# Router logits taken from the unnormalised x, x turned once into the output banks, and the norm weight multiplied in where columns are copied

## The chip, the cores and the metric

The kernel runs on one core of one Trainium2 chip. The time is device microseconds of one execution. The core has a matrix engine (TensorE, in the profile PE, its weight loads PEld), VectorE (DVE), ScalarE (ACT), GpSimd (POOL) and SyncE (SP), which here only issues transfers; all transfers share 16 DMA engines. All data is fp32.

## What is computed

One layer of a hybrid decoder over 264 tokens (256 of a prompt, 8 samples) of width 1024. The change touches only the part behind the mixer: the residual, the norm before the experts, the router and the experts' inputs.

```python
x = x + m                                        # m: output of the mixer
h = _rmsnorm(x, norm_ffn_g)                      # y = x * rsqrt(mean(x*x) + EPS) * g
gp = softmax(h @ w_router_group)                 # 4 groups, the best one is taken
el = (h @ w_router_expert)                       # 32 experts, 8 of them in the best group
tv, ti = top_k(softmax(el of that group), 2)     # two experts for a token
for e in range(32):
    a = silu(h @ w_expert_gate[e]) * (h @ w_expert_up[e])
    out = out + combine[:, e:e + 1] * (a @ w_expert_down[e])
x = x + out                                      # then a last RMSNorm, and the output
```

Every expert has three matrices of 1024x512 or 512x1024, 2 MB each: 192 MB for the 32 experts.

## The kernel before

**Stages.** Up to about 332 us the kernel runs the mixer. Its last projection, label `wo`, makes eight 128x264 tiles; VectorE adds each to the turned residual `xT` (features on partitions, L1404). The router, the sorting of tokens and the first gather fill 332 to 351 us. Then 16 pairs of experts follow, 26.8 us each on TensorE: `gate`, `up` (both in `hidden`, L2007), `turn`, `down` (L2045) and `combine` (L2053).

**The router before.** VectorE also makes `hT[d] = xT[d] * g` (L1407), which raises `xg_ready`. TensorE's `route` multiplies `hT` with the router's weights `wrout` (L1918) into `logits`. ScalarE squares `xT`, VectorE sums the squares, and TensorE sums them over partitions into one column for each token tile (L1929). From it ScalarE and GpSimd make the factor `rs` for each token. `turn_groups` turns `hT` to token-major (L1581, six groups of four transposes), and ScalarE copies these groups times `rs` to `xrow` (L1026), which SyncE stores as `tok_rows`. In between, `seat` multiplies `xT` with the identity into banks 0 to 3 (L1933), where the experts' outputs are added up until the end; the fourth and fifth group of seats stand behind the ranks. VectorE picks the best group and two experts by `first_max` (five steps each, L1422 to L1426), makes `member`, TensorE counts ranks from it (`ranks`, L1957 to L1961), and VectorE turns the ranks into positions and the selection matrices `sel0` (L1450, L1451).

**The first gather.** `first_block` (L1971) multiplies `xrow` with `sel0`, half by half, into two banks. `m_gathered` counts the halves. Here ScalarE copies the columns of the first pair of experts to `xe` (L1075, L1076) and all columns to `xall` (L1077). For pairs 1 to 15 GpSimd copies from `xall` to `xe` (L793).

**The weights' ring.** SyncE's queue is written by hand: it streams the experts' matrices into a ring of 20 half slots of 1 MB (`RING`, `load_half`, `load_slot`, L556, L559, L569), and its instructions wait in order. The places that the mixer frees last are four half slots over the arrays `gates` and `x_early`; halves 16 to 19 go there. Half 18 lies over `xT`, half 17 over the router's small arrays (freed by `smalls_done`, L1475), half 19 over `xrow` (freed by `m_gathered` 2 and by `rows_kept`, the landing of `tok_rows`). From half 20 on a load waits for the TensorE step that read its place last. The queue there is:

```python
load_half(16)
sp.wait_ge(*misc.read(("ht", 5)))
... two stores of tok_rows
sp.wait_ge(seated, 1); sp.wait_ge(x_kept, 1)
load_half(18)
sp.wait_ge(quad_ready, 1)
... two stores of tok_quad
sp.wait_ge(smalls_done, 1)
load_half(17)
sp.wait_ge(rows_kept, 32); sp.wait_ge(m_gathered, 2)
load_half(19)
```

Ahead of load 7 (one whole slot) SyncE also stores `hT` to `h_rows` (L591). Only a branch for overfull experts reads it back, and that branch is not taken.

## Time and profile before

| | |
|---|---|
| median of 3 runs | 806.62 us (805.08 to 806.87) |
| the profiled execution's own time | 806.2 us |
| its span | 804.2 us |
| TensorE busy | 773.9 us (96%) |
| VectorE, ScalarE, GpSimd busy | 234.4, 176.4, 97.2 us |
| moved by DMA | 267.90 MB, mean 333 GB/s over the span |
| chain that ended last, by engine | PE 81%, DMA 13%, DVE 2% |

A span is what the profiler saw between the first and the last instruction; the time of an execution is 2.0 us more here. A small "idle before" of TensorE does not say that transfers have slack: read the share of the DMA engines in the same stretch beside it. L12 is line 12 of the kernel before.

### The profile page before, as it was taken

What the parts mean: (1) busy time and instruction counts of PE and PEld (TensorE: products, weight loads), DVE (VectorE), ACT (ScalarE), POOL (GpSimd) and SP (SyncE); (2) the same over time, 40 slices, a digit from 0 to 9 for tenths busy, and PEclk for the clock granted to TensorE, in tenths of its full rate; (3) what the DMA queues carried; (4) which work ended last, traced back from release to release, by engine and by line L of the source; (5) the groups of instructions that cost most, each with busy time, mean ns of one, the idle gap of its engine ahead of it and who ended that gap; (6) DMA issues with size and microseconds to landing.
All of it is one profiled execution on the core that took longest, in us unless ns stands there. A gap on an engine that the chain in (4) does not pass through costs nothing.

```text
span 804.2 us, 10140 instructions
## 1 busy us (share of the span) xinstructions
PE 773.9 (96%) x4170; PEld 445.8 (55%) x4170; DVE 234.4 (29%) x533; ACT 176.4 (22%) x321; POOL 97.2 (12%) x128
## 2 busy tenths in 40 slices
PE   8999999999999999999999999999999989999995
PEld 7888887888888888863333333333333333333331
DVE  4099869482550322441101110111011101101112
ACT  3104333657544101231111001100110010010011
POOL 5300064523300000001101000001000000000001
PEclk9999999999999999999999999999999999999998
DMA  9845586578849974499999999999999999999993
GB/s 329 244 149 187 164 239 207 181 214 169 276 148 365 398 259 191 162 360 430 423 429 417 426 429 425 429 426 427 427 429 427 430 427 429 425 428 419 421 409 149
DMA packets 76374, 267.90 MB, mean 333 GB/s; under 512 B 5598, under 2 KB 37578, under 8 KB 63647
## 3 DMA queue, kind: packets, MB, share of 16 engines
q1 hardware_dynamic: 74402, 264.13, 84.3%
q10 hardware_dynamic: 1461, 1.45, 0.6%
q0 software_dynamic: 464, 1.64, 0.5%
q8 instruction: 35, 0.57, 0.3%
q14 instruction: 12, 0.10, 0.0%
HBM read 259.13 MB, written 8.55 MB: 333 GB/s over the span
## 4 chain that ended last, share of the span: by engine, by line
PE 81%; DMA 13%; DVE 2%; issue 1%; ACT 1%; POOL 1%; SPq 0%; DVEq 0%
PE bank L2007 23%; PE bank L1630 23%; PE bank L2045 10%; PE bank L1903 7%; PE bank L2053 6%; DMA slots<-in_w_expert_gate_dram 5%; DMA x_early<-in_w_expert_gate_dram 5%; DMA slots<-in_w_expert_down_dram 2%; PE bank L1850 2%; PE bank L1740 1%; DMA slots<-in_w_in_dram 1%; PE bank L2034 1%; DVE x_early L1488 1%; PE bank L1971 1%; PE bank L1662 1%
## 5 line engine op out<-in xcount | busy, mean ns | idle before, releaser
L1630 PE MATMUL bank<-hT,slots 128*128 128x264 f32 x832 | 189.6, 387 | 0.0
L2007 PE MATMUL bank<-slots,hT 128*64 128x512 f32 x624 | 177.9, 601 | 2.1 <-DMA slots<-in_w_expert_gate_dram 2.1
L1630 PEld LDWEIGHTS bank<-hT,slots 128*128 128x128 f32 x832 | 156.6, 190 | 26.8 <-issue 0.6
L1488 DVE TENSOR_TENSOR x_early<-x_early,bank 128x512 f32<-128x512 f32 x16 | 11.0, 688 | 376.6 <-PE bank L2007 376.6
L2007 PEld LDWEIGHTS bank<-slots,hT 128*64 128x64 f32 x624 | 55.1, 138 | 91.1 <-issue 86.5
L2045 PE MATMUL bank<-slots,wrep 128*64 128x512 f32 x304 | 85.4, 595 | 4.7 <-ACT wrep L1053 4.0
L2007 PE MATMUL bank<-slot,hT 128*64 128x512 f32 x208 | 81.4, 593 | 0.0
L793 POOL COPY hT<-x_early 128x512 f32 x30 | 17.9, 623 | 369.3 <-PE bank L2007 286.2
L2053 PE MATMUL bank<-hT,diag 128*128 128x512 f32 x128 | 59.2, 605 | 0.2 <-ACT hT L1065 0.2
L2045 PEld LDWEIGHTS bank<-slots,wrep 128*64 128x64 f32 x304 | 26.0, 137 | 49.3 <-issue 39.6
L1228 DVE SCALAR_TENSOR_TENSOR slot<-slot,rows_buf 128x256 f32<-128x256 f32 x120 | 49.4, 488 | 0.0
L1053 ACT COPY wrep<-bank 128x512 f32<-128x512 f32 x16 | 9.4, 586 | 169.6 <-PE bank L2034 169.6
L2045 PE MATMUL bank<-slot,wrep 128*64 128x512 f32 x112 | 42.7, 596 | 2.3 <-ACT wrep L1053 2.3
L2007 PEld LDWEIGHTS bank<-slot,hT 128*64 128x64 f32 x208 | 24.9, 137 | 34.9 <-issue 33.7
L2007 PE MATMUL bank<-x_early,hT 128*64 128x512 f32 x96 | 42.3, 594 | 1.5 <-DMA x_early<-in_w_expert_gate_dram 1.5
L2053 PEld LDWEIGHTS bank<-hT,diag 128*128 128x128 f32 x128 | 22.9, 189 | 35.7 <-issue 35.1
L2007 PE MATMUL bank<-gates,hT 128*64 128x512 f32 x96 | 42.5, 594 | 0.0
L1065 ACT COPY hT<-bank 128x512 f32<-128x512 f32 x31 | 16.7, 589 | 113.3 <-PE bank L2045 113.3
L1048 ACT ACTIVATE x_early<-bank 128x512 f32<-128x512 f32 x16 | 16.9, 1057 | 109.2 <-PE bank L2007 109.2
L1903 PE MATMUL bank<-gates,slots 128*128 128x264 f32 x128 | 30.1, 390 | 0.0
L1903 PE MATMUL bank<-x_early,slots 128*128 128x264 f32 x128 | 28.6, 386 | 0.0
L1903 PEld LDWEIGHTS bank<-x_early,slots 128*128 128x128 f32 x128 | 24.3, 190 | 4.2
(301 smaller groups left out, 759.6 us busy)
## 6 DMA issues: line engine op xcount, KB each, us to landing
slots<-in_w_expert_gate_dram SPq DMA_DIRECT2D x15, 2048.0 KB, 23.2
slots<-in_w_expert_up_dram SPq DMA_DIRECT2D x15, 2048.0 KB, 28.7
slots<-in_w_expert_down_dram SPq DMA_DIRECT2D x15, 2048.0 KB, 29.7
slots<-in_w_in_dram SPq DMA_DIRECT2D x13, 2048.0 KB, 10.0
slots<-in_w_expert_gate_dram SPq DMA_DIRECT2D x10, 1024.0 KB, 26.2
slot<-in_w_expert_gate_dram SPq DMA_DIRECT2D x5, 2048.0 KB, 27.7
slot<-in_w_expert_up_dram SPq DMA_DIRECT2D x5, 2048.0 KB, 23.7
slot<-in_w_expert_down_dram SPq DMA_DIRECT2D x5, 2048.0 KB, 34.1
```

What stands on the lines that cost most here:

```text
L793: pool.tensor_copy(xe[:, :, e * SLOTS:(e + 1) * SLOTS], xall[:, :, bass.ds(at[e], SLOTS)]).then_inc(m_xe, 1)
L1048: se.activation(act.rearrange("s (f c) -> s c f", f=FT), bank[GATE][:, :].rearrange("s (c f) -> s c f", f=FT), ACT.Silu).then_inc(m_silu, 1)
L1053: se.copy(actT, bank[4][:, :].rearrange("p (f s) -> p f s", f=FT)).then_inc(m_actT, 1)
L1065: se.copy(ytok[:, 512 * i:512 * (i + 1)], bank[4 + i][:, :]).then_inc(m_ytok, 1)
L1228: i = dve.scalar_tensor_tensor(conv[:, c, 0:SEQ], upad[:, c, j:j + SEQ], taps[:, c, j:j + 1], conv[:, c, 0:SEQ], ALU.mult, ALU.add)
L1488: dve.tensor_tensor(act.rearrange("s (f c) -> s f c", f=FT), act.rearrange("s (f c) -> s f c", f=FT), bank[UP][:, :].rearrange("s (c f) -> ...
L1630: last = mm(out, w[:, a, t * P:(t + 1) * P], (hT if c else xgain)[:, a, :], start=(a == 0), stop=(a == KT - 1))
L1850: last = mm(bank[proj.bank(("ya", d))][:, 0:T], w[:, c, d * P:(d + 1) * P], conv[:, c, :], start=(c == 0), stop=(c == CT - 1))
L1903: last = mm(bank[proj.bank((label, d))][:, 0:T], w[:, a, (d % 4) * P:(d % 4 + 1) * P], src[:, a, :], start=(a == 0), stop=(a == KT - 1))
L2007: last = mm(out[sl, :], xe[:, a, sl], expert_view(p, kind, e, a // 2)[:, a % 2, :], start=(a == 0), stop=(a == KT - 1))
L2045: last = mm(bank[4 + i][sl, :], actT[:, f, sl], expert_view(p, 2, e, f)[:, 0, 512 * i:512 * i + 512], start=(f == 0), stop=(f == FT - 1))
L2053: return mm(bank[Y_BANKS[t][i]][:, :], wc[:, t * P:(t + 1) * P], ytok[:, CHUNK * i:CHUNK * (i + 1)], start=False, stop=stop)
```

## The change

The norm's weight g is multiplied into `wrout` once (128x288, on VectorE, before the first `wo` tile is taken), so that `route` reads `xT` itself. `hT`, its eight multiplications and the store `h_rows` are gone. `xT` is turned once, by transposes, straight into banks 0 to 3, where it stays as the residual; ScalarE takes the rows for `xrow` from those banks. Only the 8 samples are turned into the ring of banks 6 and 7. The sum over partitions is made 128 columns wide instead of one. `xrow` now lacks g; so g comes in again where columns are copied to `xe`: on VectorE for pair 0 (`first_columns`), on GpSimd for pairs 1 to 15, where the copy becomes a multiplication. g in the features' order (`g_by`, 128x8) comes by a small transfer. The choice of two experts is made with VectorE's `max` (eight largest of a row) and a key built from the experts' numbers. In SyncE's queue halves 18, 19 and 17 are loaded in another order and after other waits.

```diff
@@ SyncE
-                if c == WO + 1:
-                    sp.wait_ge(xg_ready, KT)
-                    sp.dma_start(h_rows[:, :, :], hT[:, :, :]).then_inc(h_stored, 16)
                 sp.wait_ge(proj.ready, proj.written(stream[c][1]))
                 load_slot(n)
+                if n == 5:
+                    sp.dma_start(g_by, ins["norm_ffn_g"][0].rearrange("(p a) -> p a", p=P)).then_inc(g_by_in, 16)
             load_half(16)
-            sp.wait_ge(*misc.read(("ht", 5)))
-            sp.dma_start(tok_rows[0:SEQ, :].rearrange("(t p) d -> p t d", p=P), xrow[:, 0:2, :]).then_inc(rows_kept, 16)
-            sp.dma_start(tok_rows[SEQ:T, :], xrow[0:NB, 2, :]).then_inc(rows_kept, 16)
-            sp.wait_ge(seated, 1)
+            sp.wait_ge(misc.ready, misc.written(("ht", 5)))
             sp.wait_ge(x_kept, 1)
             load_half(18)
+            sp.wait_ge(row_made, 4)
+            sp.dma_start(tok_rows[0:SEQ, :].rearrange("(t p) d -> p t d", p=P), xrow[:, 0:2, :]).then_inc(rows_kept, 16)
+            sp.wait_ge(*misc.read(("ht", 5)))
+            sp.dma_start(tok_rows[SEQ:T, :], xrow[0:NB, 2, :]).then_inc(rows_kept, 16)
             sp.wait_ge(quad_ready, 1)
...
-            sp.wait_ge(smalls_done, 1)
-            load_half(17)
             sp.wait_ge(rows_kept, 32)
             sp.wait_ge(m_gathered, 2)
             load_half(19)
+            sp.wait_ge(smalls_done, 1)
+            load_half(17)
             load_half(NR)
@@ GpSimd
                 for e in range(2):
-                    pool.tensor_copy(xe[:, :, e * SLOTS:(e + 1) * SLOTS], xall[:, :, bass.ds(at[e], SLOTS)]).then_inc(m_xe, 1)
+                    pool.tensor_tensor(xe[:, :, e * SLOTS:(e + 1) * SLOTS], xall[:, :, bass.ds(at[e], SLOTS)],
+                                       g_by[:, :].unsqueeze(2).broadcast_to([P, KT, SLOTS]), ALU.mult).then_inc(m_xe, 1)
@@ ScalarE
-            for i in range(6):
+            for i in range(4):
                 t, half = i // 2, i % 2
...
+                se.wait_ge(y_seated, i + 1)
+                se.activation(xrow_by[:, t, :, SLOTS * half:SLOTS * half + SLOTS],
+                              bank[Y_BANKS[t][half]][:, :].rearrange("p (q a) -> p a q", a=KT), ACT.Copy,
+                              scale=rs[:, t:t + 1]).then_inc(row_made, 1)
...
-            se.wait_ge(h_stored, 16)
-            se.wait_ge(offs_ready, 1)
-            second = se.value_load(offs[0:1, 1:2], min_val=0, max_val=SLOTS)
             for j in range(2):
-                se.wait_ge(m_gathered, j + 1)
+                se.wait_ge(first_xe, 2 * j + 2)
                 src = bank[GATHER[j]][:, :].rearrange("p (a c) -> p a c", a=4)
-                se.copy(xe[:, 4 * j:4 * j + 4, 0:SLOTS], src[:, :, 0:SLOTS]).then_inc(first_xe, 1)
-                se.copy(xe[:, 4 * j:4 * j + 4, SLOTS:], src[:, :, bass.ds(second, SLOTS)]).then_inc(first_xe, 1)
                 se.copy(xall[:, 4 * j:4 * j + 4, 0:P], src).then_inc(m_xall, 1)
@@ VectorE
+            dve.wait_ge(wrout_in, 32)
+            dve.tensor_tensor(wrout[:, :, :], wrout[:, :, :], vec[:, 60:60 + KT].unsqueeze(2).broadcast_to([P, KT, NG + NE]), ALU.mult).then_inc(router_ready, 1)
...
-                dve.wait_ge(*proj.read(("wo", d)))
-                dve.tensor_scalar(hT[:, d, :], xT[:, d, :], vec[:, 60 + d:61 + d], None, ALU.mult).then_inc(xg_ready, 1)
...
+            def first_columns(j):
+                dve.wait_ge(m_gathered, j + 1)
+                src = bank[GATHER[j]][:, :].rearrange("p (a c) -> p a c", a=4)
+                gain = g_by[:, 4 * j:4 * j + 4].unsqueeze(2).broadcast_to([P, 4, SLOTS])
+                dve.tensor_tensor(xe[:, 4 * j:4 * j + 4, 0:SLOTS], src[:, :, 0:SLOTS], gain, ALU.mult).then_inc(first_xe, 1)
+                dve.tensor_tensor(xe[:, 4 * j:4 * j + 4, SLOTS:], src[:, :, bass.ds(second, SLOTS)], gain, ALU.mult).then_inc(first_xe, 1)
@@ TensorE
-                pe.wait_ge(xg_ready, a + 1)
+                pe.wait_ge(*proj.read(("wo", a)))
...
+            def seat(t, i):
+                for c in range(4):
+                    last = mm(bank[Y_BANKS[t][i]][:, c * P:(c + 1) * P], xT[:, 4 * i + c, t * P:(t + 1) * P], ident[:, :],
+                              start=(c == 0), stop=(c == 3), is_transpose=True)
+                last.then_inc(y_seated, 1)
```

`first_columns(0)` stands on VectorE behind `quad_ready`, `first_columns(1)` behind the flag and ahead of the steps that end in `smalls_done`; a register load of an offset stands before both.

On TensorE, the place is the stretch from the sum over partitions to the first gather. Before (`hT` and `x_early` are the normalised and the raw x, `gates` holds `member`, the 1-column product is the end of the sum):

```order
L1929 MATMUL bank<-ones,rows_buf 128x1 x2
L1929 MATMUL bank<-ones,rows_buf 8x1
L1581 MATMUL bank<-ident,hT 128x128 x8
L1933 MATMUL bank<-ident,x_early 128x128 x4
L1581 MATMUL bank<-ident,hT 128x128 x8
L1933 MATMUL bank<-ident,x_early 128x128 x4
L1581 MATMUL bank<-ident,hT 8x128 x8
L1957 MATMUL bank<-gates,tri 128x64
L1958 MATMUL bank<-gates,ones 128x64
L1959 MATMUL bank<-gates,ones 128x96
```

Now:

```order
L1945 MATMUL bank<-ident,x_early 128x128 x4
L1953 MATMUL bank<-ones,rows_buf 128x128 x2
L1953 MATMUL bank<-ones,rows_buf 8x128
L1945 MATMUL bank<-ident,x_early 128x128 x12
L1967 MATMUL bank<-ident,x_early 8x128 x8
L1977 MATMUL bank<-gates,tri 128x64
L1978 MATMUL bank<-gates,ones 128x64
L1979 MATMUL bank<-gates,ones 128x96
L1980 MATMUL bank<-gates,tri 128x32
L1981 MATMUL bank<-gates,ones 128x32
L1989 MATMUL bank<-x_early 128x128 x24
```

The sixteen transposes of `hT` and eight of the sixteen seat products ahead of the ranks have become sixteen transposes; the eight seat products that stood between the ranks and the gather (L1971 before, L1989 now) are gone from there.

On VectorE, the choice of the experts, from the masked logits on. Before, the second `first_max` and the start of the third (`gates` holds all small arrays):

```order
L1422 TENSOR_REDUCE gates<-gates 128x3
L1423 TENSOR_TENSOR gates<-gates 128x96
L1424 TENSOR_TENSOR gates<-gates,desc 128x96
L1425 TENSOR_REDUCE gates<-gates 128x3
L1426 TENSOR_TENSOR gates<-desc,gates 128x96
L1434 SCALAR_TENSOR_TENSOR gates<-gates 128x96
```

Now, the whole choice up to `member` (L1442):

```order
L1432 MAX gates<-gates 128x8 x3
L1435 SCALAR_TENSOR_TENSOR gates<-gates,desc 128x32
L1436 SCALAR_TENSOR_TENSOR gates<-gates,desc 128x32
...
L1438 SCALAR_TENSOR_TENSOR gates<-gates 128x96
L1440 MAX gates<-gates 128x8 x3
L1442 TENSOR_TENSOR gates<-gates 128x96
```

Twelve dependent steps of 96 elements (five, one, five and `member`) have become three `max`, six steps of 32 elements that don't wait for each other, one of 96, three `max` and `member`.

On SyncE, the queue from load 6 on (L569 and L559 are loads of weights; the L559 into `gates` is half 16, the one into `x_early` half 18):

```order
-L569 DMA slots<-in_w_expert_gate_dram 128x4096
-L591 DMA h_rows<-hT 128x2112
-L569 DMA slots<-in_w_expert_gate_dram 128x4096
+L592 DMA x_early<-in_norm_ffn_g_dram 128x8
+L569 DMA slots<-in_w_expert_gate_dram 128x4096 x2
 L559 DMA gates<-in_w_expert_up_dram 128x2048
-L596 DMA tok_rows<-x_early 128x2x1024
-L597 DMA tok_rows<-x_early 8x1024
 L559 DMA x_early<-in_w_expert_up_dram 128x2048
+L598 DMA tok_rows<-x_early 128x2x1024
+L600 DMA tok_rows<-x_early 8x1024
```

Behind the two stores of `tok_quad` the queue has half 17 (into `gates`) and half 19 (into `x_early`): before 17, then 19; now 19, then 17.

One store of 1056 KB is gone, half 18 has moved ahead of the stores of rows, and half 19 ahead of half 17.

## Rows read from the trace of the kernel before

**Rows 1.** Chain that ended last, its end: start us, us, what.

```profile
770.86 18.95 DMA slots<-in_w_expert_down_dram
...
789.86 1.94 PE bank L2045 x8
...
798.01 0.66 DVEq L1536
```

**Rows 2.** Waits of TensorE from 250 us on: total us, times, longest.

```profile
PE bank L2007 <- DMA slots<-in_w_expert_gate_dram: 2.1, 1, 2.1
...
PE bank L2007 <- DMA x_early<-in_w_expert_gate_dram: 1.5, 1, 1.5
...
PE bank L2045 <- DMA slots<-in_w_expert_down_dram: 0.6, 1, 0.6
```

**Rows 3.** Windows: engines' busy us, PEclk, DMA share, GB/s at a row's end.

```profile
334.00:350.00 16.00, 15.27 (x114) 14.26 (x114) 11.42 (x52) 7.82 (x18) 0.88 (x1) 0.89 0.99 380
350.00:352.00 2.00, 2.00 (x15) 1.02 (x15) 1.94 (x4) 1.25 (x4) 0.00 (x0) 1.00 0.50 62
352.00:786.00 434.00, 416.74 (x1896) 146.28 (x1894) 46.45 (x81) 46.83 (x71) 24.57 (x41) 1.00 1.01 425
```

**Rows 4.** Timeline of SyncE's DMA issues: start us, us.

```profile
332.59 0.34 SPq L591 DMA_DIRECT2D h_rows<-hT  x1
...
341.49 0.38 SPq L596 DMA_DIRECT2D tok_rows<-x_early  x1
...
349.53 0.34 SPq L559 DMA_DIRECT2D gates<-in_w_expert_up_dram  x1
```

**Rows 5.** DMA issues by line: KB each, us to landing.

```profile
h_rows<-hT SPq DMA_DIRECT2D x1, 1056.0 KB, 4.9
```

**Rows 6.** Chain that ended last, from router to first gather.

```profile
332.21 0.37 DVE hT L1407
...
332.62 0.92 PE bank L1918 x6
...
333.59 0.70 PE bank L1929 x6
...
334.30 1.60 PE bank L1581 x8
...
339.74 0.87 PE bank L1581 x8
...
340.61 0.17 PE bank L1957 x2
...
344.52 6.17 PE bank L1971 x48
```

**Rows 7.** Timeline of VectorE and ScalarE in the router.

```profile
335.09 0.25 DVE L1422 TENSOR_REDUCE gates<-gates 128x3 f32<-128x96 f32 x1
...
335.73 1.27 ACT L1026 ACTIVATE x_early<-bank,rs 128x512 f32<-128x512 f32 x2 [1.00 <-POOL rs L772]
...
338.29 0.26 DVE L1436 TENSOR_TENSOR gates<-gates 128x96 f32<-128x96 f32 x1
...
348.92 0.19 DVE L1472 SCALAR_TENSOR_TENSOR gates<-gates 128x32 f32<-128x32 f32 x1
```

**Rows 8.** Windows with the granted clock low.

```profile
336.00:338.00 2.00, 2.00 (x11) 2.00 (x11) 1.76 (x7) 0.99 (x2) 0.00 (x0) 0.50 0.90 313
```

**Rows 9.** Chain: 30 matmuls of L2007 after two waits, and pair 1's first.

```profile
381.61 13.88 PE bank L2007 x64
...
650.90 8.78 PE bank L2007 x30
...
709.62 7.08 PE bank L2007 x30
```

**Rows 10.** GpSimd by form: busy us, mean ns.

```profile
L714 POOL TENSOR_TENSOR slots<-slots,wrep 120x512 f32<-120x512 f32 x2 | 2.5, 1264 | 7.1 <-DMA wrep<-in_conv_dw_w_dram 7.1
```

**Rows 11.** Timeline of GpSimd before pair 1.

```profile
378.96 1.16 POOL L793 COPY hT<-x_early 128x512 f32 x2 [16.19 <-ACT x_early L1041]
```

More of the change, by code:

```diff
@@ L227, in hybrid_layer @@
         gmax, gpos, gsum, gval = small(1), small(1), small(1), small(1)
-        elm, eq, elm2 = (small(NE) for _ in range(3))
+        elm, key, elm2 = (small(NE) for _ in range(3))
         oh = flat(6 * NE).rearrange("p (k a n) -> p k a n", k=2, a=3)
@@ L231, in hybrid_layer @@
         oh1, oh2 = oh[:, 0], oh[:, 1]
-        e1, p1, e2, p2, ed, er, den, rec = (small(1) for _ in range(8))
+        ed, er, den, rec = (small(1) for _ in range(4))
+        top, chosen = (flat(24).rearrange("p (a n) -> p a n", a=3) for _ in range(2))
         comb, member = small(NE), small(NE)
@@ L763, in _ @@
             pool.memset(dflat[:, T:], 0.0).then_inc(c_const, 1)
-            pool.wait_ge(proj.ready, proj.written(("wo", KT - 1)))
-            pool.wait_ge(xg_ready, KT)
+            pool.wait_ge(*proj.read(("wo", KT - 1)))
             pool.tensor_copy(x_samples, xT[:, :, SEQ:T]).then_inc(x_kept, 1)
@@ L1928, in _ @@
             for i, (t0, m) in enumerate(TOK_TILES):
-                last = mm(bank[misc.bank("ms")][0:m, i:i + 1], rstd[:, t0:t0 + m], ones[:, 0:1], start=True, stop=True)
+                last = mm(bank[misc.bank("ms")][0:m, i * P:(i + 1) * P], rstd[:, t0:t0 + m], ones[:, 0:P], start=True, stop=True)
             last.then_inc(M_ready, 1)
-            def seat(t, i, last=False):
-                for c in range(4):
-                    turned = mm(bank[Y_BANKS[t][i]][:, c * P:(c + 1) * P], xT[:, 4 * i + c, t * P:(t + 1) * P], ident[:, :],
-                                start=(c == 0 and not last), stop=(c == 3 and last))
-                return turned
             def seat_samples(x):
@@ L1941, in seat_samples @@
                        start=False, stop=False, tile_position=(0, at))
-            def beside_rows(t, half):
-                if t and half == 0:
-                    pe.wait_ge(*proj.read(("wo", KT - 1)))
-                    seat(0, t - 1)
-            turn_groups(misc, "ht", hT, beside_rows)
+            for t, i in ((0, 1), (1, 0), (1, 1)):
+                seat(t, i)
+            for half in range(2):
+                misc.before_write(pe, ("ht", 4 + half))
+                out = bank[misc.bank(("ht", 4 + half))]
+                for c in range(4):
+                    last = tr(out[0:NB, c * P:(c + 1) * P], xT[:, 4 * half + c, SEQ:T], ident[:, :])
+                last.then_inc(M_ready, 1)
             pe.wait_ge(member_ready, 1)
@@ L2146, in _ @@
                     for i in range(2):
-                        seat(t, i, last=True).then_inc(y_sum, 1)
+                        for c in range(4):
+                            last = mm(bank[Y_BANKS[t][i]][:, c * P:(c + 1) * P], xT[:, 4 * i + c, t * P:(t + 1) * P], ident[:, :],
+                                      start=False, stop=(c == 3))
+                        last.then_inc(y_sum, 1)
                 mm(bank[GATE][:, 0:PART], ident[:, :], sample_sum, start=True, stop=False)
```

103 lines of the change are left out of this document (58 added, 45 removed).

## The prediction

> **What bounds the kernel now.** I read the end of the chain that ended last first, because a change in the middle counts only by what it does to the end. There the last load of expert weights is issued at 770.86, lands 18.95 us later, and TensorE starts on it at 789.86 [rows 1]. One half slot is 1.05 MB, which takes 2.5 us at the rate below, so those 19 us are a queue: the DMA engines, not the issue, are late. Then the windows: from 352 to 786 the DMA share is 1.01 at 425 GB/s, while TensorE is busy for 416.7 of 434 us, nearly full as well [rows 3]. The waits show how close the two are: behind 250 us TensorE waited for weights three times, 2.1, 1.5 and 0.6 us [rows 2]. The third is the last load. So the transfers are the bound by a little: the end is the moment at which the stream becomes continuous, plus a fixed volume over a fixed rate, plus a tail from 789.86 on that the change leaves alone. TensorE is some 4 us behind them.
>
> The stream becomes continuous late. From 334 to 350 the share is 0.99 but only at 380 GB/s, and from 350 to 352 the queue is nearly dry: share 0.50, 62 GB/s [rows 3]. It starts again with half 17, issued at 349.53 when `smalls_done` came [rows 4]. Half 19 waits for the end of the first gather, 344.52 + 6.17 = 350.69 [rows 6], and follows it while half 17 is still moving.
>
> **What the change does to TensorE and VectorE (the time of the first gather's end).**
> Removed multiplication of `hT`: the last logits waited for its 0.37 us at 332.21 [rows 6]; they start at 332.2 in place of 332.62, a gain of 0.4. The g in `wrout` costs a VectorE operation of 288 elements, some 0.45 us, under the first tile of `wo`, for which VectorE waits anyway: nothing.
> TensorE up to the ranks, before: 340.61 - 332.62 = 8.0 us [rows 6]. Now: logits 0.9; the sum, 0.7 for six narrow passes [rows 6], which I keep for 128 columns; sixteen transposes; eight small ones. Eight transposes took 1.60 us at granted clock 0.50 (0.20 each) and the eight small ones 0.87 at full clock (0.11 each) [rows 6, 8]. So sixteen and eight cost 1.8 + 0.9 at the full clock, 3.2 + 1.6 if all of it is at half. Half speed lasted for part of it only, so I take 1.4 us on top at most. TensorE is free at 332.2 + 0.9 + 0.7 + 2.7 = 336.5, or 337.9.
> VectorE up to `member`, before: 335.09 to 338.55, 3.5 us, for twelve steps of 0.29 [rows 7]. Now: a step of 32 elements is 0.19 us [rows 7], back to back I take 0.15; `max` has no row, and I price it like such a step (bounds: 0.1, and 0.3 like a step of 96). Three `max` 0.5, six steps 1.0, one of 96 0.3, three `max` 0.5, `member` 0.3: 2.6 us, bounds 2.3 to 3.5. `member` is ready at 338.55 - 0.4 - 0.9 = 337.2. The two `is_equal` behind it (0.5 us) lie under TensorE's ranks.
> The ranks thus start at 337.2 if TensorE keeps its clock, at about 338.0 if not: 3.4 or 2.6 us earlier than 340.61. From there to the end of the gather it is 350.69 - 340.61 = 10.1 us in the same steps. ScalarE must have made six rows by then: pairs of them take 1.27 [rows 7], begun at about 335.9 they end at 339.7, ahead of the gather. The gather would end at 347.3 or 348.1.
>
> **The clock.** The seats between ranks and gather are gone, so TensorE now has nothing for about 2.6 us there (340.61 plus 1.2 of ranks to 344.52, less 0.1). After its wait of 2.1 us the 30 matmuls of L2007 took 8.78 us, after the wait of 1.5 us the same 30 took 7.08 [rows 2, 9]: one stretch at the low clock cost 1.7 us. The low level was also granted from 336 to 338, behind the narrow products of the router [rows 8]; that is 1.2 of 2.4 GHz. A gap of 2.6 us is longer than the one that cost 1.7, so I give the gather a good half chance to pay the 1.7.
> The Trainium skill, page "TensorE: Matmul & The Clock Gate", section on the HAM clock gate, says the same thing as a rule: after idleness the array gets half its pulses, and a monitor that runs free of the program decides, so that it differs from run to run; its formula for the penalty (throttled time times one half) is what rows 9 show. By that rule the seats' work was worth more than nothing where it stood, which speaks against this change. Were the rule certain to bite both times, the gather would end at 349.8.
>
> **What it does to the transfers.** Removed: a store of 1056 KB [rows 5], 1.08 MB, 2.5 us of stream at 425 GB/s. Load 7 goes out some 1.2 us earlier, since it stood behind the store issued at 332.59 [rows 4] and behind the multiplication that the store waited for. Both would be worth 3.7 us if the stream were continuous from there. It isn't. Load 7, half 16, half 18 and the rows are 5.3 MB, 13 to 14 us at 380 to 425 GB/s: begun at about 332.5 they are through at 346. The next load is now half 19, and its wait is the end of the gather, 347.3 to 349.8. The room that the store leaves turns into an idle gap in front of half 19. What counts is when the stream starts again: 349.53 before, the gather's end now. The gather's gain g (350.69 less the new end) is thus worth only g - 1.16 (350.69 less 349.53). `rows_kept` is no later: rows are through at 346, and their landing has a microsecond or two.
> Half 17 behind it needs `smalls_done`. That comes after `first_columns(1)`: two copies out of PSUM with g, about 0.45 each, then about 1.1 us of small steps, so 2.0 us behind the gather. Half 19 covers 2.5 us: no second gap, with 0.4 to spare.
> The register load on VectorE (the one at the end of the kernel took 0.66 [rows 1]; bounds 0 and 1.3) delays `quad_ready` but stands in the 3 us in which the gather's first half runs.
> GpSimd: 128x512 as a product costs about 1.26 instead of 0.58: 120x512 took that, and two copies 1.16 [rows 10, 11]. For pair 1: 378.96 + 2.5 = 381.5, the gate starts at 381.61 [rows 9]: 0 to 0.3 us on TensorE, which has slack. Later pairs have 5 us and more.
> The small transfer of g stands where the DMA engines are free: nothing.
>
> **Sum**, against the profiled execution's 806.2, which is 0.4 under the median of 806.62: g is 3.4 with no low clock, 2.6 or 1.7 with one stretch, 0.9 with both. End: -2.2; -1.4 or -0.5; +0.3.
>
> **Forecasts and rivals.**
> Main case, one stretch at the low clock, 0.40: -0.9, so 805.7 by the median (804.9 to 806.4 for its own terms).
> No low clock in the way, 0.25: -2.2, 804.4. For it: the sum is now 128 columns wide, which keeps TensorE busier; against it: the gap of 2.6 us.
> Both, 0.15: +0.3, 806.9.
> Rival 1, the transfers are not the bound or the store's 2.5 us do count, 0.08: then TensorE's 2.6 to 3.4 or the stream's 3.7 us come through, 803.3. Against it: rows 1 and the dry window.
> Rival 2, slower, 0.08: VectorE. `smalls_done` now stands behind the gather, and SyncE's whole queue behind half 17 waits for it. Decisive point: 2.5 us behind the gather. If the products with the broadcast g, the register load or the small steps take longer, each microsecond more is one of stream lost. With both low clocks (+0.3) and 2 us over that point it is +2.3, 808.9.
> Rival 3, nothing of the router's part gets shorter since something else (ScalarE's rows, the width of the sum) ends last, 0.04: g = 0, +1.2, 807.8.
>
> **How the numbers follow.** A measurement here tells 0.2%, 1.6 us, from no change. Faster than that: most of the second case and rival 1, 0.25 x 0.8 + 0.08 = 0.28, with a little of the main case's lower end 0.31. Slower: rival 2 and some of the third case and rival 3, 0.12. The same: 0.57. The range from 803.6 to 808.0 leaves out half of rival 1, rival 2 and some noise.
>
> **What would show it.** The DMA share of the stretch ahead of half 19's issue: a clear gap, longer than before. The issue of half 19 within 0.1 us of the gather's last product, half 17 some 2.0 behind. `member` about 1.3 us earlier; the ranks 2.6 to 3.4. The granted clock in the gather: 0.5 somewhere in it, and the gather then nearer 7.9 than 6.2 us. From there on share 1.0, and TensorE's waits for weights over 5 us in sum instead of 4.2. I am wrong if the end moves by more than the moment at which the stream starts again, if that moment is set by `smalls_done`, or if there is no gap in the transfers ahead of half 19.

## The result, and the profile of the changed kernel

The changed kernel took 808.57 us, median of 22 executions (804.86 to 812.95); the kernel before took 805.81 (804.95 to 806.87, 22 executions beside them). The ratio is 1.0036, with a 95% interval from 1.0026 to 1.0047: slower by 2.8 us, which is small but clear of the noise. The median is outside the range of 803.6 to 808.0, and it moved the other way: my 805.7 stood for 0.9 us less than the 806.62 that I had as the median before. The spread has grown too, from 1.9 us to 8.1, and it goes with TensorE's mean granted clock: twelve executions with 0.990 to 0.993 took 804.9 to 808.6 us, ten with 0.982 to 0.987 took 809.0 to 813.0.

The profiled execution took 810.2 us, its span is 808.3 us, 4.1 longer than before. The end of the chain that ended last (start us, us, what) answers to the first of [rows 1]:

```profile
775.27 18.61 DMA slots<-in_w_expert_down_dram
```

The last load lands at 793.88 where it landed at 789.81, 4.07 later. So the whole difference stands ahead of that landing, and nothing behind it moved. The windows that answer to [rows 3] (same columns); the dry stretch, which moved, has a row of its own:

```profile
334.00:350.00 16.00, 12.68 (x71) 11.27 (x70) 10.24 (x50) 7.02 (x16) 0.88 (x1) 0.68 0.80 315
350.00:354.00 4.00, 4.00 (x18) 2.94 (x18) 0.83 (x3) 0.04 (x1) 0.00 (x0) 0.50 0.00 0
354.00:786.00 432.00, 413.31 (x1876) 147.19 (x1872) 53.32 (x86) 46.90 (x71) 41.66 (x41) 1.00 1.01 423
```

Behind 354 us the DMA share is 1.01 again, at 423 GB/s (425 before). Between 350 and 354 the transfers stand still, share 0.00, and the granted clock is 0.50. SyncE's issues in that place answer to [rows 4]:

```profile
336.91 0.33 SPq L559 DMA_DIRECT2D x_early<-in_w_expert_up_dram  x1
338.42 0.38 SPq L598 DMA_DIRECT2D tok_rows<-x_early  x1
...
353.21 0.35 SPq L559 DMA_DIRECT2D x_early<-in_w_expert_up_dram  x1
355.00 0.35 SPq L559 DMA_DIRECT2D gates<-in_w_expert_up_dram  x1
```

The stream restarts with half 19 at 353.21. It restarted at 349.53 before [rows 4]: 3.7 us of the 4.1. What released half 19 is the first gather, on TensorE's timeline (start us, us, what, idle before it); this answers to the end of [rows 6]:

```profile
337.42 0.43 PE L1977 MATMUL bank<-gates,tri 128*128 128x64 f32 x2 [0.54 <-DVE gates L1442]
...
341.67 11.47 PE L1989 MATMUL bank<-x_early 128*128 128x128 f32 x48 [2.78 <-DVE x_early L1460]
353.07 5.46 PE L2025 MATMUL bank<-slots,hT 128*64 128x512 f32 x16
```

The ranks start at 337.42, 3.2 us earlier than before [rows 6], and the gather at 341.67, 2.9 earlier. Then the same 48 products take 11.40 us (341.67 to 353.07) in place of 6.17. The granted clock (the third figure from the end of a row) says why:

```profile
338.00:340.00 2.00, 0.89 (x7) 0.68 (x6) 0.90 (x4) 1.98 (x4) 0.00 (x0) 0.92 0.96 406
340.00:342.00 2.00, 0.33 (x1) 0.36 (x2) 1.82 (x7) 1.99 (x7) 0.00 (x0) 0.50 0.99 406
352.00:354.00 2.00, 2.00 (x10) 1.16 (x10) 0.83 (x3) 0.04 (x1) 0.00 (x0) 0.50 0.00 0
354.00:356.00 2.00, 2.00 (x8) 0.69 (x6) 1.81 (x7) 1.83 (x2) 0.00 (x0) 0.50 0.89 225
356.00:358.00 2.00, 2.00 (x10) 0.59 (x8) 1.93 (x5) 0.00 (x0) 0.00 (x0) 0.81 1.10 377
```

The clock fell to 1.2 GHz near 339.7 (0.92 is 0.3 us of 2 at half), while TensorE had nothing to do, and was back at 2.4 GHz near 356.8. TensorE's waits for weights grew from 4.2 to 5.8 us in sum (total us, times, longest; to [rows 2]):

```profile
PE bank L2025 <- DMA slots<-in_w_expert_gate_dram: 2.2, 1, 2.2
PE bank L2025 <- DMA x_early<-in_w_expert_gate_dram: 1.9, 1, 1.9
PE bank L2025 <- DMA slot<-in_w_expert_gate_dram: 1.5, 1, 1.5
...
PE bank L2063 <- DMA slots<-in_w_expert_down_dram: 0.2, 1, 0.2
```

On VectorE (to [rows 7]) the choice of the experts and what follows it:

```profile
334.88 0.38 DVE L1432 MAX8 gates<-gates 128x8 f32<-128x32 f32 x3
...
337.11 0.26 DVE L1442 TENSOR_TENSOR gates<-gates 128x96 f32<-128x96 f32 x1
...
344.77 0.17 DVE L1475 TENSOR_REDUCE gates<-gates 128x3 f32<-128x12 f32 x1 [2.02 <-issue]
```

The last line is the step behind the register load: 2.0 us in which VectorE waited for nothing that the profile shows.

### The profile page after: what moved, and what is told of

It is laid out like the page before. It is cut to its first block, busy times and chain, and to the rows that moved or that the text cites. A ratio compares the mean times of both kernels' runs of the same rounds, so it can differ in the third digit from the quotient of the medians.

```text
span 808.3 us, 10073 instructions
## 1 busy us (share of the span) xinstructions
PE 774.6 (96%) x4138; PEld 448.4 (55%) x4138; DVE 239.9 (30%) x534; ACT 174.8 (22%) x317; POOL 115.0 (14%) x128
## 4 chain that ended last, share of the span: by engine, by line
PE 79%; DMA 14%; DVE 3%; issue 2%; ACT 1%; POOL 1%; ACTq 0%; DVEq 0%; SPq 0%; POOLq 0%
PE bank L2025 23%; PE bank L1647 22%; PE bank L2063 10%; PE bank L1920 7%; PE bank L2071 6%; DMA x_early<-in_w_expert_gate_dram 5%; DMA slots<-in_w_expert_gate_dram 5%; DMA slots<-in_w_expert_down_dram 2%; PE bank L1867 2%; PE bank L1989 1%; DMA slots<-in_conv_dw_w_dram 1%; PE bank L2052 1%; DVE x_early L1510 1%; PE bank L1679 1%; ACT wrep L1058 1%
## 5 line engine op out<-in xcount | busy, mean ns | idle before, releaser
L792 POOL TENSOR_TENSOR hT<-x_early 128x512 f32<-128x512 f32 x30 | 35.3, 1198 | 353.6 <-PE bank L2025 273.2
```

The lines of the kernel that those rows point to most:

```text
L792: pool.tensor_tensor(xe[:, :, e * SLOTS:(e + 1) * SLOTS], xall[:, :, bass.ds(at[e], SLOTS)], g_by[:, :].unsqueeze(2).broadcast_to([P, KT, ...
```

## The experiments

Theory: the change brings the gather 2.9 us forward, but empties TensorE for 2.8 us ahead of it; the granted clock falls there in most executions, the gather gets longer, and as the stream restarts only at the gather's end, each microsecond of it reaches the end of the kernel. Rivals: the lost store, the order of halves 19 and 17, or the gather being slow for a reason other than the clock.

All times are medians in us over the executions in brackets. A ratio is to the kernel before, executed beside them on the same chip: 805.73 for experiments 1 to 4 (804.0 to 809.2, 31 executions), 805.60 for 5 to 8 (803.9 to 809.3, 30) and 805.84 for 9 (804.7 to 807.2, 13). Behind the changed kernel the rows of the table stand in the order of the experiments. The changed kernel was measured on yet another occasion, so the ratios are the fair way to set it beside the others; a difference of medians is good to half a microsecond at best.

| kernel | us | ratio, 95% |
|---|---|---|
| changed | 808.57 (22) | 1.0036 [1.0026, 1.0047] |
| changed + 8 covering products | 804.34 (11) | 0.9982 [0.9974, 0.9991] |
| before, without its cover | 807.71 (8) | 1.0051 [1.0024, 1.0079] |
| before, no `h_rows` store | 805.28 (11) | 0.9995 [0.9986, 1.0004] |
| cover, half 17 first | 804.94 (11) | 0.9991 [0.9980, 1.0002] |
| changed, dense operand in the gather | 807.36 (12) | 1.0028 [1.0016, 1.0040] |
| changed + 4 covering products | 806.91 (12) | 1.0018 [0.9994, 1.0042] |
| cover, rows ahead of half 18 | 804.50 (12) | 0.9986 [0.9976, 0.9995] |
| cover, early stream | 802.60 (7) | 0.9966 [0.9953, 0.9980] |
| early stream, no cover | 806.83 (10) | 1.0021 [1.0005, 1.0036] |

**1. Cover the gap.** The changed kernel, with eight products of constants between the ranks and the gather, into a bank that nobody reads.

```diff
             mm(ranks[:, 3 * NE:], ones[0:NB, 0:P], member[0:NB, 2, :], ...).then_inc(ranked, 1)
+            pe.wait_ge(exp_in, 1)
+            for _ in range(8):
+                mm(bank[4][:, P:2 * P], ones[:, 0:P], ident[:, :], start=True, stop=True)
```

> The changed kernel, with eight 128x128 products of constants between the ranks and the first gather on TensorE, where the two seats stood before. Theory (the granted clock): in the changed kernel TensorE has nothing for 2.8 us there, the clock falls to the low level and stays low through the whole gather; the eight products (2.05 us) keep it up. The gather then takes about 6.2 us in place of 11.4, ends near 348, half 19 goes out there, and the time is 803.5 to 804.5 with a spread as small as that of the kernel before (805.8). Rival 1 (VectorE's copies with g, its register load, or the queue's new order cost the time): the time stays at 808 to 809. Rival 2 (the low clock comes from the narrow products further ahead): partly better, some executions still at 808 and more.

It took 804.34 us, 4.2 less than the changed kernel and 1.4 less than before. TensorE and SyncE in its trace:

```profile
338.05 2.05 PE L1984 MATMUL bank<-ident,ones 128*128 128x128 f32 x16
340.90 6.17 PE L1992 MATMUL bank<-x_early 128*128 128x128 f32 x48 [0.80 <-DVE x_early L1460]
```

```profile
348.31 0.35 SPq L559 DMA_DIRECT2D x_early<-in_w_expert_up_dram  x1
349.15 0.35 SPq L559 DMA_DIRECT2D gates<-in_w_expert_up_dram  x1
```

The gather is at 6.17 us again, the clock stays at its full level until behind the last landing, and that landing is at 787.62. Eight products that compute nothing turn a loss into a gain, and rival 1 (804.3 is not 808) and rival 2 (no execution at 808 or more) are out: the loss is the clock's. Half 19 goes out 1.2 us after the gather's end at 347.07. SyncE's waits say for what (total us, times, longest):

```profile
SPq L559 <- DMA tok_rows<-x_early: 1.2, 1, 1.2
```

**2. Uncover the kernel before.** Its two seats of the second token tile, which stood between the ranks and the gather, are moved ahead of the ranks (as eight transposes); nothing else changes.

```diff
+            for i in range(2):
+                for c in range(4):
+                    last = mm(bank[Y_BANKS[1][i]][:, c * P:(c + 1) * P], xT[:, 4 * i + c, P:2 * P], ident[:, :],
+                              start=(c == 0), stop=(c == 3), is_transpose=True)
+            last.then_inc(seated, 1)
             pe.wait_ge(member_ready, 1)
...
-            seat(1, 0)
-            seat(1, 1).then_inc(seated, 1)
```

> The kernel before, with only the two seats of the second token tile moved from between ranks and gather to a place ahead of the ranks, as eight transposes (0.9 us). Nothing else of the change. Theory (granted clock): TensorE now has nothing for some 2.7 us ahead of the gather, the clock falls in most executions and the gather takes 8 to 11 us: 808 to 811, widely spread, and the lowest near 806.5. Rival (the seats' place is indifferent, the cost comes from other parts of the change): the ranks move by 0.9 us at most, 805.8 to 806.7, spread as before.

807.71 us: 2.0 over before, with five executions from 806.2 to 808.1 and three from 812.7 to 814.1. The gap, without anything else of the change, makes the old kernel slower and scattered. But its profiled execution (807.3 us) is one of the five: the gap is there, the clock stayed up in it, and the gather took 6.17 us (first row; the second is a later one of the chain that ended last):

```profile
344.26 6.17 PE L1974 MATMUL bank<-x_early 128*128 128x128 f32 x48 [2.71 <-DVE x_early L1451]
360.31 8.49 PE bank L2010 x32
```

For a second trace of the same kernel the expectation was:

> The kernel before with its two last seats moved ahead of the ranks, once more, for a second trace. Its first trace had the gap of 2.7 us with the clock at full; three of its eight executions took 812.7 to 814.1. Theory: in a share of executions the clock falls in the gap and the gather takes 9 to 11.5 us in place of 6.17; such an execution shows 810 us or more, the others 806.2 to 808.1 with a gather of 6.2 us. Rival: the executions at 813 have another cause, so a time of 810 or more comes with a gather of 6.2 us.

807.41 us and again a gather of 6.17 us:

```profile
344.55 6.17 PE L1974 MATMUL bank<-x_early 128*128 128x128 f32 x48 [2.71 <-DVE x_early L1451]
```

So no trace shows one of the three from the inside. Their mean granted clocks were 0.986 to 0.988, those of the other five 0.993 to 0.996: less clock goes with the time, but that it was lost in the gather is not shown. What the two traces do show is a clock that fell later, near 360 us: the second 32 gate and up products of pair 0 took 8.5 us (360.31 above) where they took 7.04 in the kernel before. Experiment 3 comes back to this.

**3. The store alone.** The kernel before without the store of `hT`; as the branch that reads it isn't taken, the outputs don't depend on it.

```diff
-                if c == WO + 1:
-                    sp.wait_ge(xg_ready, KT)
-                    sp.dma_start(h_rows[:, :, :], hT[:, :, :]).then_inc(h_stored, 16)
```

> The kernel before without the store of 1056 KB to h_rows and without the waits for it (the branch for overfull experts, which is not taken, would lack it). Theory (the stream has a dry window behind it, and starts again when smalls_done comes): no change, 805.8 within 0.5. Rival (every byte that the stream carries counts, since the DMA engines set the end): 2.5 us less, 803.3.

805.28 us, 0.45 less than before, and not told apart from it: by the ratio's interval it is between 1.1 us less and 0.3 more, and the rival's 2.5 us are out. The stretch from 346 to 350 (columns as in [rows 3]) in the kernel before, and then without the store:

```profile
346.00:350.00 4.00, 4.00 (x33) 3.64 (x33) 3.50 (x18) 1.14 (x3) 0.00 (x0) 1.00 0.97 385
```

```profile
346.00:350.00 4.00, 4.00 (x32) 3.40 (x32) 3.64 (x15) 1.47 (x5) 0.00 (x0) 1.00 0.59 163
```

The DMA share falls from 0.97 to 0.59: the store's 2.5 us have become a hole in front of half 17, as I had said. A megabyte less is worth little or nothing where the next load waits for a semaphore.

This trace (of 806.73 us, the slowest of the eleven) also shows something that I had not looked for. Its restart, half 17 at 348.46, is 1.1 us earlier than before, and yet its last load lands 0.7 us later, at 790.55. Behind the first half of pair 0 the clock fell for 3.4 us, near 360.4, and the second 32 gate and up products took 1.7 us more (first the kernel before, then this one):

```profile
360.38 7.04 PE bank L2007 x32
```

```profile
359.32 8.74 PE bank L2000 x32
```

SyncE's loads wait for steps of TensorE there: between 354 and 400 us it waited 28.2 us for gate and up products, 26.5 before, and the load that it issued at 388.72 before goes out at 389.36, although the stream had started 1.1 us earlier. In front of it the stream has a second hole (again the kernel before, then this one):

```profile
388.00:390.00 2.00, 2.00 (x12) 0.72 (x10) 0.00 (x0) 1.08 (x1) 0.00 (x0) 1.00 1.06 446
```

```profile
388.00:390.00 2.00, 2.00 (x12) 0.61 (x10) 0.00 (x0) 0.68 (x1) 0.00 (x0) 1.00 0.43 174
```

The same stretch of low clock in pair 0, between 356.6 and 363.8 us, is in seven of the thirteen traces, with and without the cover (experiments 2, twice, 3, 4, 6, 7 and 9), and the hole near 390 in four of these (experiments 2, twice, 3 and 9). So a mean granted clock does not say where the clock was low, and what comes behind the gather moves the end too, by a microsecond or two.

**4. The order of halves 17 and 19**, with the cover in place.

```diff
             sp.wait_ge(rows_kept, 32)
             sp.wait_ge(m_gathered, 2)
-            load_half(19)
-            sp.wait_ge(smalls_done, 1)
-            load_half(17)
```

and `load_half(17)` with its wait goes ahead of `rows_kept`.

> e1_cover, but half 17 (which waits for smalls_done, about 2 us behind the gather's end) is loaded ahead of half 19 again, so that the stream of weights starts again 2 us later, with nothing changed on TensorE. Theory (the end follows the moment at which the stream starts again, one for one): 2.0 us above e1_cover, some 806. Rival (TensorE sets the end, the transfers have slack): as e1_cover.

804.94 us, 0.6 more than experiment 1 where 2.0 were expected. Half 17 went out at 349.82, 2.25 us behind the gather's end, where half 19 had gone out 1.24 behind it in experiment 1, having waited for the rows' landing: 1.0 later by that measure and not 2.0. The sign is right, the size was too large: putting 19 ahead of 17 is no part of the loss, it gained some 0.6 if anything.

**5. Is it what the gather multiplies?** The changed kernel with `ones` in place of `sel0` in the gather.

```diff
-... xrow_by[0:m, t, 4 * j + c, :], sel0[0:m, t, :],
+... xrow_by[0:m, t, 4 * j + c, :], ones[0:m, 0:P],
```

> The changed kernel, the gap ahead of the gather as it is, but the gather's products take a tile of ones as moving operand in place of the selection matrix (so no tokens are selected, and the experts' inputs are sums over all tokens). Shapes, counts and waits are the same. Question: why does the clock, once low, stay low for the whole gather (11.4 us in the changed kernel) although TensorE is busy. Theory A (the selection matrix is nearly all zeros, and that counts as little work): the clock rises within the gather, which takes 8 to 9 us; the time is 805.5 to 807. Theory B (it is the kind of stretch: 128 columns behind a weight load each, a third of them on 8 partitions): the clock stays low as in the changed kernel, 808 to 809 and as wide a spread.

807.36 us, still 1.8 over before; it is 1.2 under the changed kernel's median, but the intervals of the two ratios overlap. In its trace (of 805.25 us, the fastest of the twelve; windows, columns as in [rows 3]) the clock falls in the gap and is back near 344.2, inside the gather:

```profile
340.00:342.00 2.00, 0.78 (x4) 0.81 (x5) 1.85 (x7) 1.58 (x7) 0.00 (x0) 0.69 1.03 397
342.00:344.00 2.00, 2.00 (x11) 2.00 (x11) 0.40 (x3) 0.00 (x0) 0.00 (x0) 0.50 0.94 256
344.00:346.00 2.00, 2.00 (x16) 1.76 (x16) 1.08 (x7) 0.00 (x0) 0.00 (x0) 0.96 0.98 401
```

That looked like an answer (the data, mostly zeros, keeps the clock down), but experiment 10 takes it away: with its own data the changed kernel gets its clock back inside the gather too, in another execution.

**6. Half the cover.** As experiment 1, with `range(4)`.

> e1_cover with four products in place of eight: the gap ahead of the gather is then about 1.8 us (none: 2.8, eight: 0.8). Theory (the clock falls when TensorE does too little for too long; after a wait of 1.5 us it never fell, after one of 2.1 it did once): between the two, nearer to e1_cover: 804.3 to 805.5, with perhaps some executions at 808 and more. Rival (any gap is harmful, or the eight products help in another way than by the gap's length): near the changed kernel, 807 to 808.6.

A miss: 806.91 us, from 803.22 to 814.19, nearer to the rival's 807. Six executions with a mean granted clock of 0.994 to 0.998 took 803.2 to 807.4, six with 0.983 to 0.991 took 805.6 to 814.2. The gap left is 1.69 us, and half of the executions then have a mean clock under the 0.992 that is the lowest of the kernels with all eight products; these leave 0.80 us and gave 803.4 to 805.1 in all eleven. Where the clock was low is seen in one execution only: in the profiled one, 805.4 us, the gather was spared, and the clock fell near 356.6, behind it, which also happened with a gap of 0.80 us (experiments 4 and 7). That it fell in the gather in the slow ones is likely, not shown.

```profile
341.24 6.17 PE L1992 MATMUL bank<-x_early 128*128 128x128 f32 x48 [1.69 <-DVE x_early L1460]
```

```profile
354.00:356.00 2.00, 2.00 (x16) 1.60 (x14) 0.00 (x0) 1.05 (x1) 0.00 (x0) 1.00 1.02 430
356.00:358.00 2.00, 2.00 (x13) 1.56 (x14) 0.16 (x1) 0.00 (x0) 0.52 (x1) 0.66 0.98 412
```

**7. Rows ahead of half 18**, to take away the 1.2 us of experiment 1: `load_half(18)` moves behind the two stores of `tok_rows`.

> e1_cover with the two stores of token rows ahead of half 18 again. In e1_cover half 19 was issued at 348.3, 1.2 us behind the gather's end, because it waited for these stores to land. Theory (the end follows the start of the stream again): the stores land some 2.5 us earlier, half 19 goes out with the gather's end, 1.2 us earlier, 803.2 (0.5 to 1.2 below e1_cover). Rival (the stream's start is indifferent at this size, since e4 lost 0.6 where 1.0 was due): 804.3.

Half 19 now goes out with the gather's end (348.00, the gather from 341.75 on), so the wait is gone, but the median is 804.50, no better. The forecast of 803.2 is missed, the rival's 804.3 holds. Half 19 is only 0.3 us earlier on the clock of the trace, since the gather ended 0.85 later than in experiment 1's. And the profiled execution (805.55 us, the slowest of the twelve) did not end with a transfer: the end of its chain is pair 15's `down`, without a wait for its weights.

```profile
708.92 8.78 PE bank L2028 x30
...
784.13 7.09 PE bank L2066 x32
```

Its clock was low for 3.4 us twice behind the gather, from 358.1 and from 709.6, and each cost 1.7 us of gate products (8.74 and 8.78 us in place of 7.04 and 7.08). So TensorE is so close behind the transfers that two such stretches make it the bound. For the median execution this is not shown.

**8. Start the stream earlier.** Experiment 7, and the second expert's columns with their register load are ScalarE's work; on VectorE the small steps come ahead of its copies, so `smalls_done` no longer stands behind the gather; half 17 goes out at it, ahead of half 19.

```diff
@@ ScalarE
+            se.wait_ge(offs_ready, 1)
+            second = se.value_load(offs[0:1, 1:2], min_val=0, max_val=SLOTS)
             for j in range(2):
-                se.wait_ge(first_xe, 2 * j + 2)
+                se.wait_ge(m_gathered, j + 1)
+                for a in range(4):
+                    last = se.activation(xe[:, 4 * j + a, SLOTS:], src[:, a, bass.ds(second, SLOTS)], ACT.Copy,
+                                         scale=g_by[:, 4 * j + a:4 * j + a + 1])
+                last.then_inc(second_xe, 1)
@@ VectorE
-            first_columns(0)
...
-            first_columns(1)
...
             last.then_inc(smalls_done, 1)
+            first_columns(0)
+            step(dve.tensor_reduce(cntm[:, :], total, AX.X, ALU.max))
...
+            first_columns(1)
```

> e7, and VectorE reaches smalls_done ahead of the gather's end: the register load (1.8 us of VectorE in e1_cover) and the second expert's columns go to ScalarE, the first expert's copy with g stands behind the small steps, and half 17 is loaded at smalls_done, ahead of half 19. Half 17 then goes out near 345.5, when the queue is not yet dry, so that the stream has no gap of 3 us any more. Theory (the transfers set the end): 2 to 3 us below e1_cover, 801.5 to 802.5, and TensorE's waits for weights fall from 7.0 us to 4 to 5. Rival (TensorE sets the end): as e1_cover or e7 within 0.5.

802.60 us: 3.0 less than before, and 1.7 less than experiment 1 where 2 to 3 were expected. TensorE waited 4.9 us for weights, inside the 4 to 5 expected. The chain's end, SyncE's issues and the windows:

```profile
768.28 18.56 DMA slots<-in_w_expert_down_dram
```

```profile
345.73 0.34 SPq L559 DMA_DIRECT2D gates<-in_w_expert_up_dram  x1
347.26 0.33 SPq L559 DMA_DIRECT2D x_early<-in_w_expert_up_dram  x1
```

```profile
346.00:350.00 4.00, 4.00 (x23) 2.02 (x24) 2.09 (x7) 2.76 (x7) 0.00 (x0) 1.00 0.77 168
350.00:354.00 4.00, 4.00 (x20) 1.15 (x16) 1.63 (x4) 0.62 (x1) 0.00 (x0) 1.00 1.02 424
```

Half 17 goes out at 345.73, 3.8 us before the stream of the kernel before restarted, and the last load lands 3.0 us earlier. A hole is left all the same: 168 GB/s from 346 to 350.

**9. The same without the cover.** The eight products are taken out of experiment 8.

> The early stream (rows ahead of half 18, the second expert's columns and the register load on ScalarE, half 17 at the small steps' end ahead of half 19) without the eight covering products, so the gap of some 2.8 us of TensorE ahead of the gather is back. Theory (the price of the change is the granted clock in the gather, passed on because the stream restarts only at the gather's end): half 17 goes out near 345.5 whatever the clock does, and half 19 at the gather's end; where the gather is long (11 us) the stream is dry from 348 to 352.5 only. So the loss against the covered version is 0 to 5 us execution by execution, the median 1 to 4 us over 802.6, so 803.5 to 806.5, with a spread wider than that of the covered version (2.2 us), and always under the changed kernel's 808.6. Rival (the clock is not what the cover bought): within 0.5 us of the covered version, 802.1 to 803.1, with the same narrow spread.

806.83 us (805.2 to 810.4): 4.2 more than with the cover, 0.3 over the range that I gave; the rival's 803 is out. "Always under the changed kernel's 808.6" is missed too: four of the ten took 808.65 to 810.4. The cover is worth the same 4.2 us with either queue, so the early half 17 does not shield the end from a long gather; half 19 still waits for it. Its trace has the gap of 2.78 us and a gather of 7.76:

```profile
341.55 7.76 PE L1994 MATMUL bank<-x_early 128*128 128x128 f32 x48 [2.78 <-DVE x_early L1468]
```

```profile
340.00:342.00 2.00, 0.45 (x4) 0.48 (x5) 1.86 (x7) 1.92 (x7) 0.00 (x0) 0.99 0.97 379
342.00:344.00 2.00, 2.00 (x12) 2.00 (x11) 1.76 (x10) 0.00 (x0) 0.00 (x0) 0.50 1.10 401
344.00:346.00 2.00, 2.00 (x13) 1.77 (x11) 1.76 (x9) 0.00 (x0) 0.00 (x0) 0.65 0.94 363
```

Its last load lands at 789.57, 2.7 us later than in experiment 8's trace. Half 19 is 2.1 us later (349.38 for 347.26): 1.6 by the longer gather and 0.5 by its later start. The rest goes with a low clock in pair 0 and a second hole near 388 us, as in experiment 3: share 0.32, 86 GB/s from 388 to 390.

**10. The changed kernel once more**, for a second trace.

> The changed kernel once more, for a second trace. Theory (the clock falls in the gap ahead of the gather, and when it comes back differs between executions): the gap is again 2.7 to 2.8 us and the granted clock falls in it or in the gather; the gather takes 6.2 to 11.5 us, and the last landing follows the gather's end by 440.5 to 441.5 us whatever it is. Rival (the long gather was not the clock's doing): 11.4 us again with the clock at full.

807.79 us, and a third length of the gather:

```profile
341.59 9.35 PE L1989 MATMUL bank<-x_early 128*128 128x128 f32 x48 [2.78 <-DVE x_early L1460]
```

```profile
772.93 18.56 DMA slots<-in_w_expert_down_dram
```

```profile
342.00:344.00 2.00, 2.00 (x14) 2.00 (x13) 0.65 (x4) 0.00 (x0) 0.00 (x0) 0.62 0.99 270
344.00:346.00 2.00, 2.00 (x10) 1.77 (x10) 1.02 (x6) 0.00 (x0) 0.00 (x0) 0.50 0.96 393
346.00:348.00 2.00, 2.00 (x10) 1.78 (x10) 1.28 (x5) 0.56 (x1) 0.00 (x0) 0.50 0.57 203
348.00:350.00 2.00, 2.00 (x12) 1.88 (x12) 0.92 (x5) 0.03 (x1) 0.00 (x0) 0.68 0.00 0
```

Here the clock fell near 342.5, with the gather already running, and was back near 349.3, still in it. Two executions of one kernel, and between them the step that matters: the gather's end moved from 353.07 to 350.94, 2.1 us, and the last landing from 793.88 to 791.49, 2.4 us. From the gather's end to the last landing it is 440.8 and 440.6 us.

## Why the prediction was wrong

**Right in the main: what bounds the kernel.** The end follows the restart of the stream. From the restart's issue to the last landing it is 440.3 us before, 440.7 and 440.5 in the two traces of the changed kernel, and 439.3, 439.2, 440.1 and 440.6 in experiments 1, 4, 5 and 6. It is not as fixed as the prediction had it ("a fixed volume over a fixed rate"): 441.1 in experiment 8, and 441.7, 441.5, 442.1 and 443.3 in the four traces with a second hole near 390 us (experiments 2, twice, 3 and 9). And in the trace of experiment 7 TensorE ended last. Of rival 1, that the store counts is out by experiment 3; that the transfers are not the bound is so in one trace, that of experiment 7.

**Right: the times on VectorE and TensorE.** I had `member` ready at 337.2 and the ranks at 337.2 to 338.0; the trace has `member` from 337.11 for 0.26 us, the ranks at 337.42. The three `max` took 0.38 us where I had 0.5. The gather starts 2.9 us earlier, inside my 2.6 to 3.4. The gap of TensorE is 2.78 us, 2.6 expected. The dry stretch in front of half 19 is there, and half 19 went out 0.14 us behind the gather's last product.

**Right: rival 2 did not decide.** Half 17 left 1.8 us behind half 19, inside the 2.5 us that half 19 covers. The register load cost VectorE 2.0 us, outside my bounds of 0 and 1.3, but the gather hid it. GpSimd's products took 1.05 us each where I had 1.26.

**Wrong: the price of the low clock.** The step that failed is "one stretch at the low clock cost 1.7 us", with its "good half chance". The mechanism was in the prediction, the term was too small: the gather got longer by 5.2 us in one trace and by 3.2 in the other. I took from [rows 9] the price of one stretch, and used it as the price of every stretch. A stretch costs by its length, and lengths differ. In four traces with the gap, the gather took (less 6.17), for the time that the clock was low inside it:

| trace | clock fell, came back | low inside the gather | gather longer by | per us |
|---|---|---|---|---|
| early stream, no cover | 342.0, 345.4 | 3.4 | 1.59 | 0.47 |
| dense operand | 340.8, 344.2 | 2.9 | 1.41 | 0.48 |
| changed, second trace | 342.5, 349.3 | 6.8 | 3.18 | 0.47 |
| changed, first trace | 339.7, 356.8 | 11.4 | 5.23 | 0.46 |

(The moments are worked out from the clock's share in the 2 us windows above; the gather of the dense operand runs from 341.22 to 348.80.) My 1.7 us is what the shortest of these stretches cost: in the trace of the kernel before the clock was low for 3.4 us there. By the working of the prediction with the first trace's own gather, g is 350.69 less 353.07, -2.4, and g - 1.16 is -3.5: 3.5 us slower in place of 0.9 faster, where the last landing says 4.1. With no low clock that working gave -2.2. Experiment 1 is that case: its last load lands 2.2 us earlier than before, its median is 1.4 under. One step of it was off too, "`rows_kept` is no later": the rows landed 1.2 us behind the gather's end there, since their stores now stand behind half 18.

**And the chances.** I gave 0.25 to a gather without a low clock. Of 22 executions of the changed kernel the fastest took 804.86, while the kernel with the cover, whose trace has no low clock in the way, has its median at 804.34; so probably few executions, if any, went without. The two medians are 4.2 us apart, more than one short stretch costs, which suggests that most executions pay more than one; two traces cannot show it for 22. The Trainium skill, page "TensorE: Matmul & The Clock Gate", section on the HAM clock gate, which I had weighed, gives the penalty as the throttled time times one half, and warns that it varies from run to run. The traces agree with both: 0.46 to 0.48 per us, and 3.4, 6.8 and 17.1 us low. I had read from it the formula and not what it asks for: the length as an unknown of its own. That the seats' work was worth something where it stood, which the prediction said in words, should have been a rival with the gather's whole length as its bound: at half speed 6.17 us become at most 12.3, g is then 3.4 - 6.2 = -2.8, and the end +4.0, 810.6 us. A range that reached there would have held the median. It would not have held the slowest executions, three of which took 812.0 to 813.0; none of them was traced.

**What stays open.** What decides the execution in which the clock falls, and when it comes back, was not settled: two traces of the same kernel with the same data have 6.8 and 17.1 us, so the data alone does not. The gap alone does not either: with 2.8 us the clock fell in the gap or inside the gather in all four traces (the changed kernel's two and those of experiments 5 and 9), with 2.7 us in the kernel of experiment 2 in neither of two. What stands ahead of the gap differs (TensorE also waits 0.54 us for `member` in the changed kernel, and its sixteen seats are transposes), and no run tells these apart. Nor was it tested why the clock falls in pair 0 in seven traces and not in the other six. Whether the three executions at 813 us of experiment 2 had a long gather was not seen. Why the median of experiment 7 gained nothing is open as well.

## What to carry to other kernels

When a change takes work off an engine that then waits, ask what the work was keeping up: here eight products without any use are worth 4.2 us, because they stand in a gap ahead of the products that release the transfers. Price a low clock by the length of the stretch that could run under it, not by one stretch seen elsewhere, and bound it by the whole of the operation behind the gap. Where the transfers are the bound but one load waits for a semaphore, the time of that semaphore counts first: a megabyte less ahead of it gained 0.45 us, not told apart from nothing, and a restart 2.3 us earlier gained 1.9 (experiment 8 against 7). And before a time behind the restart is called fixed, look whether later loads wait for TensorE as well: four traces of twelve had a second hole 40 us further on. A difference of a microsecond or two between two single traces can come from there.

## What the runs showed of the hardware

With a gap of TensorE of 1.7 us the executions of one kernel lay between 803.2 and 808.8 us, and one at 814.2 (experiment 6); with 0.8 us those of each kernel stayed within 2.2 us (experiments 1, 4, 7, 8). Once low, the clock stayed at 1.2 GHz for 3.4, 6.8 or 17.1 us, the longest through 48 products in 11.4 us that left TensorE no idle time; being busy did not bring it back at once. Nor did being busy always keep it up: in seven of thirteen traces it fell for 3.4 us in pair 0, without idle time of TensorE, in the 24 products of one column or in the 32 of 512 columns behind them, and cost 1.6 to 1.7 us. A register load on VectorE held it for 2.0 us. Three `max` over 128x32 took 0.38 us, and steps of 128x32 that don't wait for each other started 0.16 apart. The two stores of rows, 1 MB and 32 KB, were issued at 337.65 and 338.76 in experiment 1, behind a half slot issued at 336.14, and SyncE, which waited for both, could go on at 348.31: 10.7 and 9.5 us after their issues.
